# Down projection in pairs of output tiles: seven block products over ten of 22 K tiles, and the moves of the turned results issued by GpSimd

## Chip, cores and metric

The kernel runs on one core of a Trainium2 chip. The metric is the device time of one launch in microseconds; lower is better.

## What is computed

One layer of a hybrid decoder over 512 prompt tokens and 32 sample tokens (8 sequences of 4), 544 tokens in all, in fp32: attention and a recurrent branch, merged and projected, then an RMS norm and a SwiGLU block. The change is in the last product of that block and in what follows it:

```
f = rmsnorm(x, g_ffn_pre)
g_, u_ = jnp.split(f @ w_gate_up, 2, axis=-1)
x = x + rmsnorm((jax.nn.silu(g_) * u_) @ w_down, g_ffn_post)
```

Here D_MODEL is 1024 and D_FF is 2816, so that `w_down` has 22 K tiles of 128 rows (KF) and 8 output tiles of 128 columns (KD).

## The kernel before

**Products.** Activations stand transposed, features on the partitions and the 544 tokens on the columns, cut into two halves of 272 (HT). Every fp32 operand is split into a high part rounded to fp32r and the low rest; a product is three matmuls, high by high, high by low and low by high (weights first). ScalarE makes the high part with a copy (`hi`, L1501), VectorE the low part with a subtraction (`lo`, L2021).

**Gate and up stage.** It already multiplies in blocks: each of NS = 20 column pairs of gate and up takes seven products of 2x2 blocks instead of eight (`product`, L1364; `gu_period` on ScalarE L1896 and VectorE L2479; `sum_5`, `sum_76`, `sum_3` make the weight sums). The products are written on 128x272 PSUM banks, and VectorE and ScalarE add and copy between them. Its result is `hid`, 22 tiles of 128x544. In the last period VectorE also splits the first two pieces of the down weights and begins with `hid_low`, which makes the low part of a hidden tile (L2443); `hid_high` (L1876) makes the high part.

**Down stage.** Each of the eight output tiles m takes 22 K tiles x 3 matmuls x 2 halves = 132 matmuls (`down`, `down_steps`, L1428). The weights of a tile come in three pieces of 8, 8 and 6 K tiles (DOWN_K) through a ring of two slots: SyncE loads (`load_down`), ScalarE and VectorE split (`down_hi`, `down_lo`), each counted by `w_in_slot`, `hi_done`, `lo_done` and `tile_done`. Tile 0 begins before the last product of the gate and up stage, and consumes the hidden tiles as they are split. Tiles 1 to 6 are a loop over pairs. Tile 7 is written out by hand in two column parts, of 288 and 256 (LAST_CUT), so that the first part's norm, turn and store begin under the second's matmuls.

**What follows a tile.** ScalarE takes the finished tile out of PSUM in a blocked order, scaled by the norm's weight, and squares it (`y_evacuate`, L1935 to L1940). VectorE turns it in blocks of 32x32 into `yz` (`y_square`, L2527) and adds the squares. SyncE then moves the turned rows to their places in `ytok` by twelve DMAs a tile: eight for the prompt, each of 256 runs of 128 bytes, four for the samples (`move_y`, L800 and L802). Two buffers `yz` alternate, so `y_square(m)` waits until the moves of tile m-2 have landed (the semaphore starts at 16, and each tile adds 192):

```python
                if not isinstance(m, int):
                    e.wait_ge(y_moved, m * 192 - 176)
                e.transpose(yz[s][:, :], yg[s][:, :]).then_inc(y_turned, 1)
```

At the end TensorE sums the squares over the features, ScalarE takes the root, and VectorE makes the output rows, token on the partition, in two halves (L2564), after `x1_back` (the residual rows, which GpSimd reads back at L960) and after the moves of tiles 0 to 6 (`y_moved`). SyncE stores them. SyncE's queue is in order: a load of weights stands behind the moves ahead of it, and the other way round.

## Time and profile before

| | us |
|---|---|
| median of three runs | 769.75 (769.42 to 770.26) |
| the profiled execution | 768.84 |
| its span, first to last instruction | 766.70 |
| TensorE matmul busy | 757.5, 99% |
| VectorE busy | 484.2, 63% |
| ScalarE busy | 357.0, 47% |
| GpSimd busy | 70.5, 9% |
| matmuls | 5954 |
| TensorE's mean granted clock | 0.997 of 2.4 GHz |

The profile is of one execution of its own. Its times are from the span's start. PE is TensorE's matmul row, PEld its weight loads, DVE VectorE, ACT ScalarE, POOL GpSimd, SP SyncE. A matmul's row is 0.29 us long but the next one begins before it ends, so the pace is read from many in a row, not from one row's length.

### The profile page before, as it was taken

Reading aid. Unit: us, or ns where it says so; the run is one execution under the profiler, and the core shown is the slowest. Engines: PE = TensorE matmul, PEld = TensorE weight load, DVE = VectorE, ACT = ScalarE, POOL = GpSimd, SP = SyncE. Lnnn points to the kernel's source line nnn. Section 1 sums busy time; section 2 is a strip of 40 time slices with the busy share of each in tenths; the row PEclk is TensorE's granted clock in tenths of the full one; section 3 lists DMA queues with packets and bytes.
Section 4 is the critical chain, followed back from the end, with each engine's and each line's share of the span. In section 5 each row is a group of like instructions: output and inputs, shape, how many; then the busy total and the mean of one; then the engine's idle time right before and its main releaser. Section 6 shows DMA issues by size and latency. Waiting matters only on the chain.

```text
span 766.7 us, 16315 instructions
## 1 busy us (share of the span) xinstructions
PE 757.5 (99%) x5954; PEld 718.4 (94%) x5954; DVE 484.2 (63%) x760; ACT 357.0 (47%) x627; POOL 70.5 (9%) x156
## 2 busy tenths in 40 slices
PE   8999999999999999999999999999999999999996
PEld 6989899899898899987899999999999999999996
DVE  7456838647656555773569887777877786232323
ACT  7334634634634632343556555554555564223322
POOL 6602102011120110021000000000000010000000
PEclk9999999999999999999999999999999999999998
DMA  9645656445454225525460333332233134434333
GB/s 263 169 110 117 162 131 139 128 104 135 129 134 104 61 74 168 175 70 181 160 194 6 106 109 109 109 108 81 85 109 109 55 127 138 107 91 111 93 91 127
DMA packets 196979, 91.68 MB, mean 120 GB/s; under 512 B 65143, under 2 KB 190539, under 8 KB 196941
## 3 DMA queue, kind: packets, MB, share of 16 engines
q1 hardware_dynamic: 193182, 84.36, 40.3%
q0 software_dynamic: 2576, 6.45, 2.5%
q8 instruction: 24, 0.39, 0.2%
q10 hardware_dynamic: 1182, 0.35, 0.2%
q14 instruction: 15, 0.11, 0.1%
HBM read 82.37 MB, written 6.81 MB: 116 GB/s over the span
## 4 chain that ended last, share of the span: by engine, by line
PE 97%; DMA 1%; POOL 1%; DVE 0%; DVEq 0%; issue 0%; ACT 0%; POOLq 0%
PE ps L975 34%; PE ps L1364 28%; PE ps L1428 17%; PE ps L1258 6%; PE ps L1332 3%; PE ps L1181 2%; PE ps L1082 1%; PE ps L1096 1%; PE ps L1114 1%; DMA strow<-in_state_h_dram 1%; PE ps L1156 1%; PE ps L1266 1%; PE ps L1067 1%; PE ps L1127 1%; POOL prow L833 0%; PE ps L1293 0%
## 5 line engine op out<-in xcount | busy, mean ns | idle before, releaser
L2021 DVE TENSOR_TENSOR w_lo<-w_raw,w_hi 128x1024 fp32r<-128x1024 f32 (+1 forms) x65 | 77.3, 1190 | 120.5 <-ACT w_hi L1501 120.2
L1501 ACT ACTIVATE w_hi<-w_raw 128x1024 fp32r<-128x1024 f32 (+1 forms) x66 | 67.8, 1029 | 122.2 <-PE ps L1428 78.1
L975 PE MATMUL ps<-xin_hi,w_hi 128*128 128x272 f32 x544 | 117.0, 296 | 0.0
L975 PE MATMUL ps<-xin_hi,w_lo 128*128 128x272 f32 x544 | 112.5, 288 | 0.0
L975 PE MATMUL ps<-xin_lo,w_hi 128*128 128x272 f32 x544 | 112.3, 288 | 0.0
L975 PEld LDWEIGHTS ps<-xin_hi,w_hi 128*128 128x128 f32 x544 | 84.8, 188 | 8.1 <-issue 7.6
L975 PEld LDWEIGHTS ps<-xin_lo,w_hi 128*128 128x128 f32 x544 | 85.4, 188 | 0.0
L975 PEld LDWEIGHTS ps<-xin_hi,w_lo 128*128 128x128 f32 x544 | 85.0, 189 | 0.0
L1428 PE MATMUL ps<-hid_hi,w_hi 128*128 128x272 f32 (+2 forms) x352 | 75.3, 289 | 0.0
L1428 PE MATMUL ps<-hid_lo,w_hi 128*128 128x272 f32 (+2 forms) x352 | 74.9, 287 | 0.0
L1428 PE MATMUL ps<-hid_hi,w_lo 128*128 128x272 f32 (+2 forms) x352 | 74.9, 287 | 0.0
L1428 PEld LDWEIGHTS ps<-hid_lo,w_hi 128*128 128x128 f32 x352 | 56.2, 188 | 0.0
L1428 PEld LDWEIGHTS ps<-hid_hi,w_hi 128*128 128x128 f32 x352 | 55.8, 188 | 0.0
L1428 PEld LDWEIGHTS ps<-hid_hi,w_lo 128*128 128x128 f32 x352 | 55.8, 188 | 0.0
L1364 PE MATMUL ps<-xq_lo,b_hi 128*128 128x272 f32 x160 | 46.6, 292 | 0.0
L1364 PE MATMUL ps<-xq_hi,a_lo 128*128 128x272 f32 x160 | 46.4, 290 | 0.0
L1364 PE MATMUL ps<-xq_lo,a_hi 128*128 128x272 f32 x160 | 46.2, 289 | 0.0
L1364 PE MATMUL ps<-xq_hi,b_hi 128*128 128x272 f32 x160 | 46.2, 288 | 0.0
L1364 PE MATMUL ps<-xq_hi,b_lo 128*128 128x272 f32 x160 | 46.1, 288 | 0.0
L1364 PE MATMUL ps<-xq_hi,c_hi 128*128 128x272 f32 x160 | 46.1, 288 | 0.0
L1364 PE MATMUL ps<-xq_hi,a_hi 128*128 128x272 f32 x160 | 46.1, 288 | 0.0
L1364 PE MATMUL ps<-xq_hi,c_lo 128*128 128x272 f32 x160 | 45.9, 287 | 0.0
(349 smaller groups left out, 1769.0 us busy)
## 6 DMA issues: line engine op xcount, KB each, us to landing
w_raw<-in_w_in_dram SPq DMA_DIRECT2D x68, 256.0 KB, 3.2
g_raw<-in_w_gate_up_dram SPq DMA_DIRECT2D x40, 256.0 KB, 3.7
w_raw<-in_w_down_dram SPq DMA_DIRECT2D x40, 256.0 KB, 2.8
u_raw<-in_w_gate_up_dram SPq DMA_DIRECT2D x20, 256.0 KB, 3.0
e_raw<-in_w_gate_up_dram SPq DMA_DIRECT2D x20, 256.0 KB, 4.2
kc<-in_cache_k_dram SPq DMA_DIRECT2D x64, 64.0 KB
vc<-in_cache_v_dram SPq DMA_DIRECT2D x64, 64.0 KB
wo_raw<-in_w_out_dram SPq DMA_DIRECT2D x12, 256.0 KB, 4.0
```

Of the source, the lines that this page charges most:

```text
L975: mm = e.matmul(ps[:, bank + h, 0:HT], wt[:, kw, :], xt[:, kx, h * HT:h * HT + HT], start=first and wt is wh and xt is xh, stop=last and ( ...
L1067: e.matmul(ps[GR * g:GR * g + GR, S_BANK, 0:PAST], q_bd[:, b, :], kcT[:, b, :], start=b < NG, stop=b >= NG, skip_group_check=True)
L1082: mm = e.matmul(ps[:, SCORE_BANK[h], score_cols(qt)], qT[rows, qt * P:(qt + 1) * P], kT[rows, 0:(qt + 1) * P], start=True, stop=True)
L1096: mm = e.transpose(ps[:, T_BANK, c0:c0 + P], lgt[:, h, l0 + kt * P:l0 + kt * P + P], ident[:, :])
L1114: mm = e.matmul(ps[DH * h:DH * h + DH, O_BANK, kt * P:SEQ], tok[:, 1, kt, DH * h:DH * h + DH], value_cols(h, kt), start=kt == 0, stop=kt = ...
L1181: mm = e.matmul(ps[:, 2 * s + h, 0:cols.stop - cols.start], w[:, k, :], x[:, k, cols], start=first and k == 0, stop=last and k == KD - 1, ...
L1258: mm = e.matmul(ps[:, o_bank(tt) + c, :], xt[:, k, tt * P:tt * P + P], wt[:, c * NHALF:(c + 1) * NHALF], start=k == K_ORDER[0] and xt is x ...
L1332: mm = e.matmul(ps[:, 4 * m + 2 * c + h, 0:HT], wt[:, k, :], xt[:, x, k % KQ, :], start=k == 0 and wt is wh and xt is xq_hi, stop=k == KD ...
L1364: mm = e.matmul(ps[:, bank, 0:HT], wt[:, k0 + k, :], xt[:, x, k, :], start=first and k == 0 and wt is wh and xt is xq_hi, stop=last and k ...
L1428: mm = e.matmul(ps[:, D_BANK[odd] + h, 0:cols.stop - cols.start], wt[:, k, :], x, start=first and k == ks[0] and wt is wh and not lo_x, st ...
L1501: e.activation((to or w_hi[s])[:, 0:k, :], w_raw[s][:, 0:k, :], ACT.Copy).then_inc(hi_done, count)
L2021: e.tensor_tensor(wl[:, 0:k, :], w_raw[s][:, 0:k, :], wh[:, 0:k, :].bitcast(F32), ALU.subtract).then_inc(lo_done, count)
```

## The change

Tiles 1 to 6 are made in three pairs (N7). K tiles 6 to 10 (from KA) and 11 to 15 (from KB), five each (SK), two output tiles and two column halves make blocks of 2x2, which take seven products instead of eight. Four sums of hidden blocks (`hs`) are made once, in and after the last period of the gate and up stage; four sums of weight blocks (`op_sums`) are made for each pair on VectorE, in place in the raw buffers. The other 12 K tiles stay plain and are added into the same banks, in four pieces of three K tiles for each output tile. A pair has 15 operands (OPS7): seven of five K tiles, eight of three, all split into one ring of three slots (`op_hi`, `op_lo`), whose slot j % 3 may be written when operand j-3 has been used. The raw plain pieces have two buffers. ScalarE copies four partial results out of PSUM (`snap`), VectorE adds five times (`c_11`, `c_21_part`, `c_12`, `c_22_21`), and the tile is taken from `c_pair` in SBUF (`y_pair`) instead of from PSUM. The loops over pairs are unrolled.

SyncE keeps the weight loads: four of five K tiles (320 KB) and eight of three (192 KB) a pair, in place of six pieces in two DMAs each. The `move_y` DMAs go to GpSimd's queue. The reads of x1 rows, which GpSimd issued in a row after the gate and up stage, now stand among the moves and wait for late operands of the third pair. `y_moved` no longer starts at 16, and `y_square(m)` waits for the moves of tiles 0 to m-1. Tiles 0 and 7 keep their matmuls; tile 7's pieces come under new counts (C_LAST).

```diff
+SK, KA, KB = 5, 6, 11
+PLAIN_K, PK = (0, 3, 16, 19), 3
+N7 = (KD - 2) // 2
+OPS7 = 15
+(OP_A11, OP_A12, OP_A22, OP_P1, OP_S2, OP_S3, OP_S1, OP_S4, OP_P2) = (0, 1, 2, 3, 7, 8, 9, 10, 11)
+C_LAST = C_DOWN + 3
+HS_0, OP_0, SUM_0, C_0 = 4, KD, 3 * NS, NS
...
+            def load_op(n, op, buf, k0, m):
+                e.dma_start(buf[:, :, :], wd[:, k0:k0 + SK, m * P:m * P + P]).then_inc(raw_in[op], 16)
+            def load_plain(n, i):
+                r = 8 * n + i
+                k0, m = PLAIN_K[i % 4], 2 * n + 1 + i // 4
+                e.dma_start(raw_p[r % 2][:, :, :], wd[:, k0:k0 + PK, m * P:m * P + P]).then_inc(raw_p_in[r % 2], 16)
+            e.wait_ge(lo_done, C_DOWN + 4)
+            load_op(0, "11", raw_11, KA, 1)
+            e.wait_ge(q2_done, NS)
+            load_plain(0, 0)
+            e.wait_ge(lo_done, C_DOWN + 5)
+            load_op(0, "12", raw_12, KB, 1)
+            load_op(0, "22", raw_22, KB, 2)
+            e.wait_ge(tile_done, C_DOWN + 5)
+            load_op(0, "21", raw_21, KA, 2)
+            load_plain(0, 1)
+            for n in range(N7):
+                o = OPS7 * n
+                for i in (2, 3, 4, 5):
+                    e.wait_ge(op_l, OP_0 + o + OP_P1 + i - 1)
+                    load_plain(n, i)
+                if n + 1 < N7:
+                    e.wait_ge(op_sum, SUM_0 + 4 * n + 4)
+                    e.wait_ge(op_l, OP_0 + o + OP_S2 + 1)
+                    load_op(n + 1, "11", raw_11, KA, 2 * n + 3)
+                    e.wait_ge(op_l, OP_0 + o + OP_S3 + 1)
+                    load_op(n + 1, "21", raw_21, KA, 2 * n + 4)
+                    e.wait_ge(op_l, OP_0 + o + OP_S1 + 1)
+                    load_op(n + 1, "22", raw_22, KB, 2 * n + 4)
+                    e.wait_ge(op_l, OP_0 + o + OP_S4 + 1)
+                    load_op(n + 1, "12", raw_12, KB, 2 * n + 3)
+                else:
+                    e.wait_ge(op_sum, SUM_0 + 4 * N7)
+                    e.wait_ge(op_l, OP_0 + o + OP_S4 + 1)
+                    for c in range(2):
+                        k0 = sum(DOWN_K[:c])
+                        load(C_LAST + c, (1 + c) % 2, wd[:, k0:k0 + DOWN_K[c], (KD - 1) * P:KD * P], DOWN_K[c])
+                for i in (6, 7):
+                    e.wait_ge(op_l, OP_0 + o + OP_P2 + i - 5)
+                    load_plain(n, i)
+                if n + 1 < N7:
+                    for i in (0, 1):
+                        e.wait_ge(op_l, OP_0 + o + OP_P2 + i + 3)
+                        load_plain(n + 1, i)
+            load(C_LAST + 2, 1, wd[:, KF - DOWN_K[2]:KF, (KD - 1) * P:KD * P], DOWN_K[2])
...
+            for m in range(KD - 3):
+                for part in range(3):
+                    move_y(m, m % 2, part)
+            e.wait_ge(op_used, OP_0 + OPS7 * (N7 - 1) + OP_S1 + 1)
+            for tt in (1, 2, 3):
                 e.dma_start(x1tok[:, tt, :], token_rows(x1_dram, tt)).then_inc(x1_back, 16)
+            for part in range(3):
+                move_y(KD - 3, 1, part)
+            e.wait_ge(op_used, OP_0 + OPS7 * N7 - 1)
+            e.dma_start(x1tok[:, 0, :], token_rows(x1_dram, 0)).then_inc(x1_back, 16)
             e.dma_start(x1tok[0:TS, TT, :], x1_dram[SEQ:T, :]).then_inc(x1_back, 16)
+            for part in range(3):
+                move_y(KD - 2, 0, part)
...
+            def block_product(n, j, bank, x, first, last):
+                e.wait_ge(op_l, OP_0 + OPS7 * n + j + 1)
+                wh, wl = op_hi[j % 3], op_lo[j % 3]
+                for k, (xh, xl) in enumerate(x):
+                    for wt, xt in ((wh, xh), (wh, xl), (wl, xh)):
+                        mm = e.matmul(ps[:, bank, 0:HT], wt[:, k, :], xt, start=first and k == 0 and wt is wh and xt is xh,
+                                      stop=last and k == SK - 1 and wt is wl, skip_group_check=True)
+                mm.then_inc(op_used, 1)
+            def plain_rest(n, j0, banks, firsts, lasts):
+                for i, k0 in enumerate(PLAIN_K):
+                    j = j0 + i
+                    e.wait_ge(op_l, OP_0 + OPS7 * n + j + 1)
+                    wh, wl = op_hi[j % 3], op_lo[j % 3]
+                    for k in range(PK):
+                        for wt, lo_x in ((wh, False), (wh, True), (wl, False)):
...
+                    mm.then_inc(op_used, 1)
...
+            for n in range(N7):
+                if n > 0:
+                    e.wait_ge(c_snap, C_0 + 4 * n)
+                block_product(n, OP_A11, U_BANK, hid_block(KA, 0), True, True)
+                if n > 0:
+                    e.wait_ge(c_done, C_0 + 5 * n - 4)
+                block_product(n, OP_A12, C11_BANK, hid_block(KB, 0), True, False)
+                if n > 0:
+                    e.wait_ge(c_done, C_0 + 5 * n)
+                e.wait_ge(hs_l, HS_0 + 1)
+                block_product(n, OP_A22, C21_BANK, sum_block(3), True, False)
+                if n > 0:
+                    e.wait_ge(c_done, C_0 + 5 * n - 2)
+                plain_rest(n, OP_P1, (C11_BANK, C12_BANK), (False, True), (True, False))
+                e.wait_ge(hs_l, HS_0 + 2)
+                e.wait_ge(c_snap, C_0 + 4 * n + 1)
+                block_product(n, OP_S2, U_BANK, sum_block(1), False, True)
+                e.wait_ge(hs_l, HS_0 + 3)
+                block_product(n, OP_S3, C22_BANK, sum_block(2), True, True)
+                e.wait_ge(hs_l, HS_0 + 4)
+                e.wait_ge(c_snap, C_0 + 4 * n + 2)
+                block_product(n, OP_S1, U_BANK, sum_block(0), False, True)
+                block_product(n, OP_S4, C12_BANK, hid_block(KB, 1), False, True)
+                e.wait_ge(c_snap, C_0 + 4 * n + 3)
+                plain_rest(n, OP_P2, (C21_BANK, C22_BANK), (False, False), (True, True))
...
-            e.wait_ge(y_free, KD)
+            e.wait_ge(c_done, C_0 + 5 * N7 - 2)
...
+            def op_high(n, j):
+                o = OPS7 * n + j
+                if o < 2:
+                    e.wait_ge(tile_done, C_DOWN + 4)
+                elif o == 2:
+                    e.wait_ge(tile_done, C_DOWN + 5)
+                else:
+                    e.wait_ge(op_used, OP_0 + o - 2)
+                if OP_P1 <= j < OP_S2 or j >= OP_P2:
+                    r = 8 * n + (j - OP_P1 if j < OP_S2 else j - OP_P2 + 4)
+                    e.wait_ge(raw_p_in[r % 2], raw_p_0[r % 2] + 16 * (r // 2 + 1))
+                    e.activation(op_hi[j % 3][:, 0:PK, :], raw_p[r % 2][:, :, :], ACT.Copy).then_inc(op_h, 1)
+                else:
+                    if j in (OP_A11, OP_A12, OP_A22):
+                        op = {OP_A11: "11", OP_A12: "12", OP_A22: "22"}[j]
+                        e.wait_ge(raw_in[op], raw_0[op] + 16 * n + 16)
+                    else:
+                        e.wait_ge(op_sum, SUM_0 + 4 * n + {OP_S1: 1, OP_S3: 2, OP_S2: 3, OP_S4: 4}[j])
+                    e.activation(op_hi[j % 3][:, :, :], raw_of(j)[:, :, :], ACT.Copy).then_inc(op_h, 1)
+            def snap(n, use, j, dst, bank):
+                e.wait_ge(op_used, OP_0 + OPS7 * n + j + 1)
+                if n > 0:
+                    e.wait_ge(c_done, C_0 + 5 * n)
+                e.activation(dst, ps[:, bank, 0:HT], ACT.Copy).then_inc(c_snap, 1)
...
+            hs_high(3, 4)
+            op_high(0, 0); op_high(0, 1)
+            hs_high(1, 4)
+            op_high(0, 2); op_high(0, 3)
+            hs_high(2, 4)
+            op_high(0, 4)
+            hs_high(0, 4)
+            for n in range(N7):
+                if n > 0:
+                    op_high(n, 2); op_high(n, 3)
+                snap(n, 1, OP_A11, c_pair[0][:, 0:HT], 2)
+                if n == 0:
+                    op_high(n, 5)
+                    y_evacuate(0, 0)
+                else:
+                    y_pair(2 * n, 0, c_pair[1], 5 * n)
+                    op_high(n, 4); op_high(n, 5)
+                for j in range(6, 10):
+                    op_high(n, j)
+                snap(n, 2, OP_S2, c_pair[1][:, 0:HT], 2)
+                op_high(n, 10)
+                snap(n, 3, OP_S3, p7_snap[:, :], 5)
+                op_high(n, 11)
+                snap(n, 4, OP_S1, c_pair[1][:, HT:T], 2)
+                op_high(n, 12); op_high(n, 13)
+                y_pair(2 * n + 1, 1, c_pair[0], 5 * n + 3)
+                op_high(n, 14)
+                if n + 1 < N7:
+                    for j in range(2):
+                        op_high(n + 1, j)
+            e.wait_ge(op_used, OP_0 + OPS7 * N7 - 1)
+            hi(C_LAST, C_LAST // 2, 1, DOWN_K[0])
+            e.wait_ge(op_used, OP_0 + OPS7 * N7)
+            hi(C_LAST + 1, (C_LAST + 1) // 2, 0, DOWN_K[1])
+            y_pair(KD - 2, 0, c_pair[1], 5 * N7)
+            hi(C_LAST + 2, (C_LAST + 2) // 2, 1, DOWN_K[2])
...
+            b11, b12 = (hid[:, KA:KA + SK, h * HT:h * HT + HT] for h in range(2))
+            b21, b22 = (hid[:, KB:KB + SK, h * HT:h * HT + HT] for h in range(2))
             q = NS - 1
+            e.wait_ge(hid_done, KB + SK)
+            e.wait_ge(a_l, NS)
+            e.tensor_tensor(hs[0][:, :, :], b12, b11, ALU.subtract).then_inc(hs_done, 1)
             up_2(q - 1, 0)
+            e.wait_ge(hs_done, HS_0 + 1)
+            e.tensor_tensor(hs[1][:, :, :], b22, hs[0][:, :, :], ALU.subtract).then_inc(hs_done, 1)
             low_b(q)
             low_c(q, 1)
             gate_1(q, 1)
-            for c in range(2):
-                lo(C_DOWN + c, c)
+            e.wait_ge(c_l, NS)
+            e.tensor_tensor(hs[2][:, :, :], b22, b12, ALU.subtract).then_inc(hs_done, 1)
             up_1(q - 1, 0)
+            lo(C_DOWN, 0)
             low_d(q, 1)
             hid_product(q - 1, hid[:, KF - 2, :])
             for k in range(2):
                 hid_low(k)
+            lo(C_DOWN + 1, 1)
             up_2(q, 1)
-            for k in range(2, EARLY):
+            for k in range(2, 4):
                 hid_low(k)
             up_1(q, 1)
+            e.wait_ge(hs_done, HS_0 + 2)
+            e.wait_ge(d_l, NS)
+            e.tensor_tensor(hs[3][:, :, :], b21, hs[1][:, :, :], ALU.subtract).then_inc(hs_done, 1)
+            for k in range(4, EARLY):
+                hid_low(k)
+            e.wait_ge(hs_done, HS_0 + 4)
+            hid_low(EARLY)
             hid_product(q, hid[:, KF - 1, :])
...
...
+            def op_sums(n):
+                e.wait_ge(raw_in["21"], raw_0["21"] + 16 * n + 16)
+                e.wait_ge(op_l, OP_0 + OPS7 * n + OP_A22 + 1)
+                e.tensor_tensor(raw_22[:, :, :], raw_21[:, :, :], raw_22[:, :, :], ALU.add).then_inc(op_sum, 1)
+                e.wait_ge(op_sum, SUM_0 + 4 * n + 1)
+                e.tensor_tensor(raw_21[:, :, :], raw_11[:, :, :], raw_21[:, :, :], ALU.subtract).then_inc(op_sum, 1)
+                e.wait_ge(op_sum, SUM_0 + 4 * n + 2)
+                e.tensor_tensor(raw_11[:, :, :], raw_22[:, :, :], raw_11[:, :, :], ALU.subtract).then_inc(op_sum, 1)
+                e.wait_ge(op_sum, SUM_0 + 4 * n + 3)
+                e.tensor_tensor(raw_12[:, :, :], raw_12[:, :, :], raw_11[:, :, :], ALU.subtract).then_inc(op_sum, 1)
...
             def y_square(m, s):
                 e.wait_ge(y_free, m + 3)
-                if not isinstance(m, int):
-                    e.wait_ge(y_moved, m * 192 - 176)
+                if m > 1:
+                    e.wait_ge(y_moved, m * 192)
                 e.transpose(yz[s][:, :], yg[s][:, :]).then_inc(y_turned, 1)
...
+            op_low(0, 0)
+            op_low(0, 1)
+            hs_low(3, 1)
+            op_low(0, 2)
+            op_low(0, 3)
+            hs_low(1, 2)
+            op_low(0, 4)
+            op_sums(0)
+            op_low(0, 5)
+            e.memset(yacc[:, :], 0.0).then_inc(consts_v, 1)
+            e.wait_ge(consts_v, 7)
             y_square(0, 0)
-            with e.Fori(0, (KD - 2) // 2) as n:
-                y_tile(n, 1)
-                y_tile(n + 1, 0)
-            lo(C_DOWN + 3 * KD - 1, (C_DOWN + 3 * KD - 1) % 2, DOWN_K[2])
+            op_low(0, 6)
+            hs_low(2, 3)
+            op_low(0, 7)
+            hs_low(0, 4)
+            for n in range(N7):
+                if n > 0:
+                    c_22_21(n - 1)
+                    op_low(n, 2); op_low(n, 3)
+                    op_sums(n)
+                    op_low(n, 4); op_low(n, 5)
+                    y_square(2 * n, 0)
+                    op_low(n, 6); op_low(n, 7)
+                c_11(n)
+                op_low(n, 8); op_low(n, 9); op_low(n, 10)
+                c_21_part(n)
+                op_low(n, 11); op_low(n, 12); op_low(n, 13)
+                c_12(n)
+                op_low(n, 14)
+                y_square(2 * n + 1, 1)
+                if n + 1 < N7:
+                    op_low(n + 1, 0); op_low(n + 1, 1)
+            lo(C_LAST, 1, DOWN_K[0])
+            c_22_21(N7 - 1)
+            lo(C_LAST + 1, 0, DOWN_K[1])
+            y_square(KD - 2, 0)
+            lo(C_LAST + 2, 1, DOWN_K[2])
```

## Rows read from the trace of the kernel before

**Rows 1.** The page's table of busy time, whole span.

```profile
PE 757.5 (99%) x5954; PEld 718.4 (94%) x5954; DVE 484.2 (63%) x760; ACT 357.0 (47%) x627; POOL 70.5 (9%) x156
```

**Rows 2.** The chain that ended last, in order of time: start, length, what.

```profile
413.57 208.33 PE ps L1364 x1656
...
623.42 3.00 PE ps L1364 x24
626.42 127.52 PE ps L1428 x1014
```

**Rows 3.** Waits, 620 to 766: total, times, longest.

```profile
ACT w_hi L1501 <- PE ps L1428: 78.1, 21, 5.2
...
DVE yz L2527 <- DMA ytok<-yz: 2.8, 4, 0.7
```

**Rows 4.** Timeline of VectorE, 596 to 642.

```profile
601.16 1.22 DVE L2400 TENSOR_TENSOR b_lo<-s_raw,b_hi 128x1024 fp32r<-128x1024 f32 x1
602.30 1.22 DVE L2400 TENSOR_TENSOR c_lo<-e_raw,c_hi 128x1024 fp32r<-128x1024 f32 x1
...
608.74 0.72 DVE L2436 TENSOR_TENSOR hid<-sl,ub 128x544 f32 x1
611.37 0.44 DVE L2422 SCALAR_TENSOR_TENSOR ub<-ub,ps 128x272 f32<-128x272 f32 x1 [1.91 <-PE ps L1364]
...
628.28 6.44 DVE L2443 TENSOR_TENSOR hid_lo<-hid,hid_hi 128x544 fp32r<-128x544 f32 x10
...
635.51 3.90 DVE L2443 TENSOR_TENSOR hid_lo<-hid,hid_hi 128x544 fp32r<-128x544 f32 x6
```

**Rows 5.** Timeline, TensorE and ScalarE: start, length, instruction, idle before.

```profile
559.72 0.29 PE L1364 MATMUL ps<-xq_hi,a_lo 128*128 128x272 f32 x1
...
560.05 0.40 ACT L1855 ACTIVATE gh<-ps 128x272 f32<-128x272 f32 x1 [0.40 <-PE ps L1364]
...
626.75 5.57 ACT L1876 ACTIVATE hid_hi<-hid 128x544 fp32r<-128x544 f32 x10
...
637.06 1.06 ACT L1501 ACTIVATE w_hi<-w_raw 128x1024 fp32r<-128x1024 f32 x1 [0.72 <-PE ps L1428]
```

**Rows 6.** DMA issues: count, size of one, median from issue to landing.

```profile
w_raw<-in_w_down_dram SPq DMA_DIRECT2D x40, 256.0 KB, 2.8
...
ytok<-yz SPq DMA_DIRECT2D x56, 32.0 KB, 2.1
...
bias_rev<-dist_shift POOLq DMA_DIRECT2D x4, 130.0 KB, 3.3
...
dist_shift<-drow POOLq DMA_DIRECT2D x4, 8.1 KB, 4.3
```

**Rows 7.** Instructions of DMA issues, SyncE's with ns min/median/max, GpSimd's with mean ns.

```profile
L800 SPq DMA_DIRECT2D ytok<-yz x56: 631/638/1180, 645.4 to 749.9; - x56
L802 SPq DMA_DIRECT2D ytok<-yz x28: 529/579/648, 657.2 to 752.5; - x28
...
L816 SPq DMA_DIRECT2D out_dram<-ytok x4: 341/364/376, 757.5 to 763.5; - x4
...
L856 POOL DMA_DIRECT2D bias_rev<-dist_shift x4 | 2.1, 554 | 4.0 <-DMA dist_bias<-drow 4.0
L960 POOL DMA_DIRECT2D x1tok<-x_dram x4 | 2.1, 528 | 252.2 <-PE ps L1364 252.2
...
L852 POOL DMA_DIRECT2D dist_shift<-drow x4 | 2.0, 509 | 1.3 <-ACT drow L1545 1.3
```

**Rows 8.** Timeline of ScalarE and VectorE at the end.

```profile
741.93 0.74 ACT L1935 ACTIVATE yg<-ps,prm 128x256 f32<-128x256 f32 x1
...
743.21 0.64 ACT L1940 ACTIVATE ysq<-ps 128x544 f32<-128x544 f32 x1
...
756.21 3.67 DVE L2564 SCALAR_TENSOR_TENSOR ytok<-ytok,ycol,x1tok 128x1024 f32<-128x1024 f32 x3 [0.47 <-DVE ycol L2557]
...
761.01 2.48 DVE L2564 SCALAR_TENSOR_TENSOR ytok<-ytok,ycol,x1tok 128x1024 f32<-128x1024 f32 x2 [0.34 <-ACT ytok L1968]
```

More of the change, by code:

```diff
@@ new lines, in _, with hs_low @@
+            e.wait_ge(d_l, NS)
[4 more added lines that the diff above has]
+            hid_low(EARLY)
+            hid_product(q, hid[:, KF - 1, :])
+            def hs_low(i, count):
+                e.wait_ge(hs_h, HS_0 + count)
+                e.tensor_tensor(hs_lo[i][:, :, :], hs[i][:, :, :], hs_hi[i][:, :, :].bitcast(F32), ALU.subtract).then_inc(hs_l, 1)
```

184 lines of the change are left out of this document (117 added, 67 removed).

## The prediction

> **What bounds the kernel now.** I read the page's table of busy time first: TensorE's matmul row is busy 99% of the span [rows 1], at full clock throughout. Then the chain that ended last, in order of time: from 413.57 it is matmuls only, one block of 1656 and, in the down stage, one of 1014 without a break in 127.52 us [rows 2]. That is 125.8 ns a matmul in both (208.33 / 1656 and 127.52 / 1014), whether neighbours change the PSUM bank or stay on it. The waits of the down stage say who waits for whom: ScalarE waits for TensorE, VectorE for ScalarE, and in tile after tile VectorE's 32x32 turn waited for the moves of the turned rows, 2.8 us in four times, which cost nothing because TensorE had work [rows 3]. So a matmul less is 125.8 ns less, as long as its operand is split in time; and a move of turned rows costs nothing only as long as nobody on the path waits for it.
>
> **Matmuls.** Tiles 1 to 6 take 2 x 22 x 6 = 264 matmuls a pair. Now a pair takes 7 x 5 x 3 = 105 in block products and 8 x 3 x 3 x 2 = 144 plain ones, 249. Three pairs: 45 fewer, 45 x 0.1258 = 5.66 us. Tiles 0 and 7 keep theirs.
>
> **The other engines' prices.** VectorE: 1024 columns 1.22 us, 544 columns 0.72, 272 columns 0.44 [rows 4], so 1.04 ns a column and 0.15 to begin; two independent ones follow each other 0.08 under that. A block operand (640 columns) is 0.82, a plain one (384) 0.55, a sum of hidden blocks (1360) 1.57. ScalarE: 1024 columns 1.06, and ten of 544 in 5.57 [rows 5]: 0.73, 0.51 and 1.35 for the same three. From the last matmul of a product to ScalarE's start I take 0.2 us from the product's last issue slot: matmul at 559.72 for 0.29, ScalarE at 560.05 [rows 5]. Per pair VectorE has 15 operands (9.1), four weight sums (each waits for the last, 4 x 0.86), five adds from the products (1.8), two turns and adds (2.8): 17 of 31.3 us. ScalarE has some 13. Neither is the bound by its sum; only order can hurt.
>
> **Front of the stage.** VectorE gets four sums of 1.57. The first fits between 609.46 and 611.37, where it was idle [rows 4]; the others push what follows. Worked forward: the second ends at 613.3, two operands and an add later the third at 617.5; an add, a piece, an operand, a product, two low parts, a piece, an add and two low parts bring VectorE to 624.3; the next add waits for its matmuls until 625.1, the fourth sum ends at 627.0, three low parts at 628.9. So the last hidden product starts 2 us later than before, at 628.9, and the low part of hidden tile 7 lands at 630.3, where TensorE wants it at 626.42 + 5 x 0.755 = 630.2 [rows 2, 4]: a stall of 0.1. After that VectorE makes a tile each 0.64 and TensorE eats one each 0.755, so the lateness isn't repeated. Bounds: 0 (the sums fall in idle time) and 0.9 (one more wait of VectorE there). I take 0.1.
>
> **Inside a pair.** Split operands go round three slots: ScalarE may make operand j when product j-3 has ended, and TensorE then has two products to do, 3.8 to 4.5 us, against 0.73 + 0.82 + 0.3 of latency. About 2 us are left for what stands before it in the two in-order queues. The tightest place is the ninth operand (index 8): VectorE first adds C11, which needs the end of product 6; 0.2 + 0.36 + 0.82 + 0.04 = 1.4 after it, inside product 7's 1.89: 0.5 to spare. The four weight sums (3.45) sit before operand 4, with 0.9 to spare. Raw weights: a plain piece is 192 KB, the nearest load row is 256 KB in 2.8 us [rows 6]; I take 2.6, and 3.2 for 320 KB; the plain pieces would have to land 1.6 later than that before TensorE waited. So 0 here; bounds 0 and 2.5 (each pair waits once for 0.8).
>
> **The step to the last tile.** ScalarE's first piece of tile 7 waits until the last but one product has been used, then 1.06 + 1.22 and latencies of 0.27 = 2.55 against that last product's 2.26: 0.3 stall. TensorE's sum: -5.66 + 0.1 + 0.3 = -5.3.
>
> **The moves.** Twelve DMAs a tile leave SP's queue (there 0.638 and 0.579 us of issue each, 2.1 to landing) and go to GpSimd's, in a fixed order with the x1 reads. SP had room, so nothing on the path gains by that; SP now carries 15 loads a pair and none of its waits is late in the schedule above. The trace has no such move from GpSimd. Nearest rows: 8 rows a DMA 0.509, 128 rows 0.528 to 0.554 [rows 7]. The prompt moves have 256 runs of 128 bytes; by those rows they are 0.58, the four sample moves 0.51. Upper bound: SP takes 0.364 for 128 long rows and 0.638 for such a move [rows 7]; the same factor 1.75 on 0.528 gives 0.92 (and 0.8 for the small ones). Lower: 0.53. Landing: 3.3 for 130 KB into SBUF, 4.3 for small ones into HBM [rows 6]; lower 2.9 (3.3 less the 0.3 or 0.4 by which SP's moves beat its 256 and 128 KB loads). I take 3.3. GpSimd's x1 issues at 626.7, beside VectorE's busiest stretch, took the same 0.53 [rows 7], so I charge nothing for VectorE beside them.
> Q, from a turn to the last of its moves landed, is then 8 x 0.58 + 3 x 0.51 + 3.3 = 9.5 us.
>
> The change also makes each turn wait until all moves of the tile right before have landed (before, those of the tile before that one: the count went from m*192 - 176 with 16 given in advance to m*192 with none). Odd to even tile is the short way: in the schedule tile 1's turn ends at 669.5 and tile 2's is due at 680.3, 10.8 for Q = 9.5. It holds, barely. If it fails, the operand queued behind the turn (index 6, a plain one) is late only after 3.2 more, since VectorE idles 1.6 there and TensorE wants it 1.6 later still.
>
> **The end** is where it doesn't hold. Tile 5's turn ends at 732.9: its plain operand 13 waits for a piece issued behind four loads of tile 7, then add, ScalarE's copies of 1.28 + 0.64 [rows 8], one operand, turn. Moves landed 742.4; only then tile 6's turn, 743.1 (its data are ready at 738.6); moves landed 743.1 + 9.5 = 752.6. The last piece of tile 7 is split by VectorE behind that turn, done 744.6, wanted 745.1: no stall. The final adds of the first half stood at 756.21 and would stand at 750.9 with TensorE's 5.3; they wait for the moves instead, until 752.65. They take 3.67, so the second half starts at 756.35, where it stood at 761.01 and TensorE would have let it start at 755.7 [rows 8]. 1.1 us of the moves' 1.7 are hidden by the slack between 756.21 + 3.67 and 761.01. End: -4.65.
>
> The Trainium skill, DMA: Bandwidth & Descriptors, section Issuing engines are not separate DMA queues, says that issuing from several engines saves only sequencer time, since all share the DMA engines; the rows agree in that SP's time wasn't on the path, and the sum has no gain for it.
> The same page, Anatomy of one DMA, puts a GpSimd DMA at 2.0 us plus bytes / 436e3, an estimate of 2.1 for 32 KB; with the 0.58 of issue that would make the landing 2.7, Q 8.9, and the whole -5.3.
>
> **Sum.** The profiled execution took 768.84 us (span 766.70); the median of the three timed runs is 769.75, 0.9 more. 769.75 - 4.65 = 765.1 us.
>
> **Rivals.**
> A. TensorE alone sets the end: the moves land in time (Q up to 9.1). For it: GpSimd's 0.53 and SP's short landing; against: landings of 3.3 and 4.3 [rows 6]. -5.3, 764.4 (764.2 to 765). Chance 0.22.
> B, mine: Q between 9.1 and 10.9 and the moves eat part of the gain: -5.2 to -1.8, 764.6 to 768. Chance 0.48.
> C. Waits inside the pairs: landing of raw pieces later by 1.6 or more, or an order that costs one wait of 0.8 or so a pair, 2.5 in all on top of B: -2.1, 767.6 (766 to 769). Against: schedule slack of 0.5 to 2.8 at every operand. Chance 0.12.
> D, other side: GpSimd's issue is as much dearer as SP's was, 0.92 and 0.8. Q = 7.4 + 2.4 + 3.3 = 13.1. The even tiles' turns wait 2.3 us, inside their 3.2; at the end the two Qs stand one behind the other: 732.9 + 13.1 + 0.8 + 13.1 + 3.7 = 763.6 for the second half against 761.0: +2.6, 772.3 (with landings of 4.3, 2 more: 774.3). It decides from Q = 11.8 on, where 732.9 + 2Q + 0.8 + 3.7 reaches 761.0. For it: no row has 256 runs from GpSimd. Against: from 8 to 128 rows the price rose by 4 to 9%. Chance 0.14.
> E. The gain isn't there (matmuls slow down by new operands or the longer code without a loop): long unlooped stretches ran at the same pace earlier, 0 to +1. Chance 0.04.
>
> **Numbers.** A difference under 0.2% (1.5 us) can hardly be told from none. Faster by more than that (under 768.2): A, nearly all of B and two thirds of C, 0.76. Same (to 771.3): a little of B, the rest of C, E and the mildest D, 0.10. Slower 0.14. The range 763.9 to 770.0 holds A, B, C and part of E; B's own is 764.6 to 768. The lower end is the bound with no stall at all (-5.66, 764.1) less the runs' scatter; above 770.0 stand D and a bit of E, 0.16.
>
> **What would show it.** Right: 5909 matmuls, 45 fewer, the chain still TensorE's up to some 753; GpSimd busy with 84 moves of 0.5 to 0.6 us; VectorE's turn of tile 6 waiting 4 us for a DMA; the first final add waiting for a DMA (about 1.7 us) and starting near 752.6; tile 7's first matmul after a gap of 0.3. Wrong: moves of 0.8 us or more from GpSimd, with waits of TensorE after each even tile's turn (C and D differ by who is waited for: a load's or a move's DMA), or a matmul pitch over 126 ns.

## The result, and the profile after

The changed kernel takes 772.16 us (median, 770.59 to 773.85) against 769.31 (768.92 to 773.07) of the kernel before on the same chips: ratio 1.0034, 95% interval 1.0028 to 1.0041. It is slower by 2.85 us; 765.1 was predicted, with a range up to 770.0. The profiled execution of the changed kernel took 772.7 us (span 770.9), 0.5 over its median. The one of before lay 0.5 under the median of its 22 runs, so the two traces stand 3.9 apart (4.2 in span) and not 2.85.

The page's table of busy time of the changed kernel, which answers to [rows 1]: 45 matmuls fewer, as counted, and TensorE busy for 2.3 us less, where 5.66 were expected.

```profile
PE 755.2 (98%) x5909; PEld 715.4 (93%) x5909; DVE 519.2 (67%) x822; ACT 376.1 (49%) x670; POOL 125.1 (16%) x240
```

The chain that ended last, in order of time (start, length, what), which answers to [rows 2]. L1531 are the products of tiles 0 and 7, L1569 the block products, L1584 the plain ones.

```profile
622.36 1.51 PE ps L1531 x12
623.87 3.00 PE ps L1467 x24
626.87 15.27 PE ps L1531 x120
642.14 5.63 PE ps L1569 x45
...
673.38 5.63 PE ps L1569 x45
...
704.62 5.63 PE ps L1569 x45
710.25 9.06 PE ps L1584 x72
719.31 1.90 PE ps L1569 x15
...
725.24 9.98 DMA raw_p<-in_w_down_dram
735.30 0.53 ACT op_hi L2105
735.86 0.57 DVE op_lo L2769
736.47 7.47 PE ps L1584 x36
743.95 13.00 PE ps L1531 x102
```

The first and the second pair take 31.24 us each (642.14, 673.38, 704.62), which is 249 matmuls at 125.5 ns, without a stall. The third takes 39.33 (704.62 to 743.95): 8.1 us are lost in it. The chain names the place: one plain weight piece, issued at 725.24, is under way for 9.98 us, and behind it stand its two splits and then TensorE.

The waits from 620 to 770 (total, times, longest), which answer to [rows 3]. ScalarE waited for that one load, VectorE for ScalarE, TensorE for VectorE:

```profile
DVE op_lo L2769 <- ACT op_hi L2105: 30.9, 14, 9.5
ACT op_hi L2105 <- DMA raw_p<-in_w_down_dram: 21.7, 7, 9.5
...
PE ps L1584 <- DVE op_lo L2769: 5.1, 1, 5.1
```

The timeline of TensorE around the stall (one row is two matmuls), and the windows of 5 us beside it (after the length: busy time of TensorE, of its weight loads, of VectorE, ScalarE and GpSimd, then the granted clock as a share of 2.4 GHz, the busy share of the DMA engines, and GB/s):

```profile
730.68 0.41 PE L1584 MATMUL ps<-hid_lo,op_hi 128*128 128x272 f32 x2
730.93 0.41 PE L1584 MATMUL ps<-hid_hi,op_lo 128*128 128x272 f32 x2
736.47 0.82 PE L1584 MATMUL ps<-hid_hi,op_hi 128*128 128x272 f32 x2 [5.13 <-DVE op_lo L2769]
737.09 0.66 PE L1584 MATMUL ps<-hid_lo,op_hi 128*128 128x272 f32 x2
737.55 0.66 PE L1584 MATMUL ps<-hid_hi,op_lo 128*128 128x272 f32 x2
...
742.53 0.42 PE L1584 MATMUL ps<-hid_lo,op_hi 128*128 128x272 f32 x2
742.78 0.41 PE L1584 MATMUL ps<-hid_hi,op_lo 128*128 128x272 f32 x2
```

```profile
725.00:730.00 5.00, 5.00 (x42) 5.00 (x41) 0.56 (x1) 0.81 (x2) 1.61 (x3) 1.00 0.88 242
730.00:735.00 5.00, 1.35 (x11) 1.12 (x9) 0.00 (x0) 0.00 (x0) 0.00 (x0) 1.00 0.83 313
735.00:740.00 5.00, 3.53 (x15) 3.53 (x16) 1.60 (x4) 3.00 (x7) 0.00 (x0) 0.57 0.03 9
740.00:745.00 5.00, 5.00 (x33) 5.00 (x32) 3.14 (x5) 2.07 (x3) 3.88 (x6) 0.75 0.19 44
```

The 8.1 us are two things. TensorE stands for 5.3 us (from 731.18, when the two matmuls of 730.93 have left their slots, to 736.47). Then a pair of matmuls takes 0.45 us instead of 0.25 until 742.5, while the granted clock is at the lower level (1.2 GHz; 0.50 in each window of 1 us from 736 to 742); the 26 matmuls from 736.47 to 742.53 take 6.1 us instead of 3.3, which is the other 2.8. The DMA columns say what went on meanwhile: the engines were busy at 0.88 and 0.83 of their share, where the 5 us ahead of these show 0.16.

Who filled them stands in the timeline of the two issuing queues:

```profile
723.18 2.02 SPq L650 DMA_DIRECT2D w_raw<-in_w_down_dram  x4
725.24 1.56 SPq L849 DMA_DIRECT2D raw_p<-in_w_down_dram  x2
```

```profile
725.26 1.61 POOL L1057 DMA_DIRECT2D x1tok<-x_dram  x3 [4.46 <-PE ps L1569]
```

SyncE issued four loads of tile 7 (256 KB each) and, 0.02 us ahead of GpSimd, the first of two plain pieces; GpSimd issued three reads of x1 (512 KB each), which the kernel before had issued at 626.72, ahead of all of this. Nine transfers, 2.9 MB, were issued from 723.18 to 726.9. Both plain pieces took 10.0 and 10.1 us, where the median of the 24 is 2.6.

The moves, as instructions (ns min/median/max) and as transfers (count, size, median to landing), which answer to [rows 7] and [rows 6]:

```profile
L1048 POOL DMA_DIRECT2D ytok<-yz x56: 702/707/743, 652.9 to 757.5; - x56
L1050 POOL DMA_DIRECT2D ytok<-yz x28: 496/512/533, 658.5 to 759.7; - x28
```

```profile
raw_p<-in_w_down_dram SPq DMA_DIRECT2D x24, 192.0 KB, 2.6
raw<-in_w_down_dram SPq DMA_DIRECT2D x12, 320.0 KB, 3.2
...
ytok<-yz POOLq DMA_DIRECT2D x56, 32.0 KB, 2.0
ytok<-yz POOLq DMA_DIRECT2D x28, 4.0 KB, 1.6
```

And the end, from the timeline of VectorE, which answers to [rows 8]:

```profile
749.88 0.74 DVE L2808 STREAM_TRANSPOSE yz<-yg 128x544 f32<-128x544 f32 x1 [3.58 <-DMA ytok<-yz]
...
761.41 3.66 DVE L2869 SCALAR_TENSOR_TENSOR ytok<-ytok,ycol,x1tok 128x1024 f32<-128x1024 f32 x3 [2.67 <-DMA ytok<-yz]
...
765.19 2.48 DVE L2869 SCALAR_TENSOR_TENSOR ytok<-ytok,ycol,x1tok 128x1024 f32<-128x1024 f32 x2
```

The sum over the two traces: the last square sums of TensorE begin at 762.56, where they stood at 759.55: 3.0 later, which is -5.66 for the matmuls, +0.2 for the front (15.27 for 120 matmuls), +8.1 for the third pair and +0.5 because the down stage began later (622.36 for 621.90), in all 3.1. The last adds stand at 765.19 against 761.01: 1.2 more than TensorE's 3.0, because the first adds had waited for the moves.

### The profile page after: what moved, and what is told of

Read it like the earlier page. It is cut to its first block, busy times and chain, and to the rows that moved or that the text cites. A ratio compares the mean times of both kernels' runs of the same rounds, so it can differ in the third digit from the quotient of the medians.

```text
span 770.9 us, 16112 instructions
## 1 busy us (share of the span) xinstructions
PE 755.2 (98%) x5909; PEld 715.4 (93%) x5909; DVE 519.2 (67%) x822; ACT 376.1 (49%) x670; POOL 125.1 (16%) x240
## 4 chain that ended last, share of the span: by engine, by line
PE 95%; DMA 2%; POOL 1%; DVE 1%; ACT 0%; SPq 0%; issue 0%; DVEq 0%; POOLq 0%; ACTq 0%
PE ps L1078 33%; PE ps L1467 27%; PE ps L1584 7%; PE ps L1361 6%; PE ps L1569 4%; PE ps L1531 4%; PE ps L1435 3%; PE ps L1284 1%; PE ps L1185 1%; PE ps L1199 1%; DMA raw_p<-in_w_down_dram 1%; PE ps L1217 1%; DMA strow<-in_state_h_dram 1%; PE ps L1259 1%; PE ps L1369 1%; PE ps L1170 1%
## 5 line engine op out<-in xcount | busy, mean ns | idle before, releaser
L1048 POOL DMA_DIRECT2D ytok<-yz x56 | 39.4, 710 | 324.4 <-DVE yz L2808 321.6
L2247 DVE TENSOR_TENSOR w_lo<-w_raw,w_hi 128x1024 fp32r<-128x1024 f32 (+1 forms) x47 | 56.9, 1211 | 51.4 <-ACT w_hi L1664 51.1
L1664 ACT ACTIVATE w_hi<-w_raw 128x1024 fp32r<-128x1024 f32 (+1 forms) x48 | 50.1, 1045 | 51.4 <-PE ps L1078 39.5
L1467 PE MATMUL ps<-xq_lo,c_hi 128*128 128x272 f32 x160 | 45.9, 287 | 0.0
L1584 PE MATMUL ps<-hid_hi,op_hi 128*128 128x272 f32 x144 | 31.1, 299 | 5.1 <-DVE op_lo L2769 5.1
L2769 DVE TENSOR_TENSOR op_lo<-raw_p,op_hi 128x384 fp32r<-128x384 f32 x24 | 13.2, 556 | 30.9 <-ACT op_hi L2105 30.9
L1986 ACT ACTIVATE a_hi<-g_raw 128x1024 fp32r<-128x1024 f32 x20 | 21.2, 1062 | 21.1 <-PE ps L1467 17.5
L1584 PE MATMUL ps<-hid_lo,op_hi 128*128 128x272 f32 x144 | 30.8, 296 | 0.0
```

What stands on the lines that cost most here:

```text
L1048: e.dma_start(prompt[:, 2 * part:2 * part + 2, d, :], yz[s][rows, c0:c0 + 2 * P]).then_inc(y_moved, 16)
L1467: mm = e.matmul(ps[:, bank, 0:HT], wt[:, k0 + k, :], xt[:, x, k, :], start=first and k == 0 and wt is wh and xt is xq_hi, stop=last and k ...
L1584: mm = e.matmul(ps[:, banks[h], 0:HT], wt[:, k, :], x, start=firsts[h] and i == 0 and k == 0 and wt is wh and not lo_x, stop=lasts[h] and ...
L1664: e.activation((to or w_hi[s])[:, 0:k, :], w_raw[s][:, 0:k, :], ACT.Copy).then_inc(hi_done, count)
L1986: e.activation(a_hi[:, :, :], g_raw[s][:, :, :], ACT.Copy).then_inc(a_h, 1)
L2247: e.tensor_tensor(wl[:, 0:k, :], w_raw[s][:, 0:k, :], wh[:, 0:k, :].bitcast(F32), ALU.subtract).then_inc(lo_done, count)
```

## The experiments

Each is compared with the kernel before, run on the same chip. Theory T: the plain piece is late because the three reads of x1 that the change puts within the third pair (the early reads, below) and tile 7's loads are in the DMA engines with it. Rivals: SyncE's order alone (R1), the moves on GpSimd (R2). The first four kernels:

**e1_order.** The last two plain pieces are issued ahead of tile 7's loads.

```
-                else:
+                for i in (6, 7):
+                    e.wait_ge(op_l, OP_0 + o + OP_P2 + i - 5)
+                    load_plain(n, i)
+                if n + 1 == N7:
                     e.wait_ge(op_sum, SUM_0 + 4 * N7)
-                    e.wait_ge(op_l, OP_0 + o + OP_S4 + 1)
                     for c in range(2):
                         ...
-                for i in (6, 7):
-                    e.wait_ge(op_l, OP_0 + o + OP_P2 + i - 5)
-                    load_plain(n, i)
```

> The changed kernel, with SyncE issuing plain pieces 6 and 7 of the third pair ahead of the first four loads of tile 7. Nothing else. Theory T (the 1.5 MB of x1 reads that GpSimd issues at 725.3 and the 1 MB of tile 7 together fill the DMA engines, and whatever weight load is behind them is late): piece 6, issued before the reads, lands in 3 us, piece 7 in 5 to 7, and now tile 7's first piece is late: TensorE stalls 1 to 3 us at the step to tile 7 or at the last operand; 766 to 768.5 us. Rival R1 (only the order in SyncE's queue matters, the x1 reads do no harm): no stall over 0.5, about 764.5. Rival R2 (moves on GpSimd are what costs): little changes, 771 to 772.

768.51 us (768.02 to 769.17), ratio 0.9987 (0.9978 to 0.9996). The stall of 5.3 is gone. Three remain: 0.47 early in the pair (at 716.4), 1.85 because the second of the two pieces still took 7.6 us beside the reads, and 0.64 at the step to tile 7. The clock kept its level. The first final adds waited 3.4 us for the moves. TensorE's stalls are T's; the time is at the upper end of what T had said.

**e2_reads.** The three early reads of x1 go behind the moves of tile 5, with the fourth.

```
-            e.wait_ge(op_used, OP_0 + OPS7 * (N7 - 1) + OP_S1 + 1)
-            for tt in (1, 2, 3):
-                e.dma_start(x1tok[:, tt, :], ...)
...
-            e.dma_start(x1tok[:, 0, :], ...)
+            for tt in (0, 1, 2, 3):
+                e.dma_start(x1tok[:, tt, :], ...)
```

> The changed kernel, with GpSimd's x1 reads of rows 1, 2 and 3 issued after the moves of tile 5, beside the read of rows 0, so that none is in flight beside the third pair's pieces. Nothing else. T: the 1 MB of tile 7 alone ahead of piece 6; it lands in 3.5 to 4.5 us instead of 10, TensorE stalls less than 0.7 us before operand 13, and the clock stays at 2.4 GHz: about 8 us off the changed kernel, 764 to 765.5. R1: piece 6 still lands after 7 us or more, a stall of 3 or more, 767 to 770. R2: 771 to 772.

772.70 us (771.3 to 773.33), ratio 1.0039 (1.0026 to 1.0053). The two pieces landed in 4.1 and 4.8 us, TensorE lost 0.7 there and 0.5 within tile 7, and yet the time didn't fall: the first final adds now waited 6.3 us for the moves of tile 6. The landing and the stall are T's; the time isn't, and lies even above R2's.

**e3_both.** Both edits.

> Both edits together. T and R1: no stall in the third pair, its 249 matmuls in 31.3 us as in the others; the end limited by the moves of tiles 5 and 6; 764 to 765.5, at most 0.7 better than with the reads moved alone under T. R2: 771 to 772.

768.67 us (768.13 to 769.25), ratio 0.9989 (0.9980 to 0.9998). TensorE is as predicted: the only gap left is 0.3 at the step to tile 7, and its last square sums begin at 754.43, 5.1 before the 759.55 of the kernel before. But the time is lower by 0.6 only, where 764 to 765.5 had been expected. GpSimd's timeline shows where the gain went:

```profile
739.98 2.14 POOL L1058 DMA_DIRECT2D x1tok<-x_dram  x4
742.10 0.50 POOL L1059 DMA_DIRECT2D x1tok<-x_dram  x1
742.91 3.53 POOL L1047 DMA_DIRECT2D ytok<-yz  x5 [0.30 <-issue]
751.75 2.10 POOL L1047 DMA_DIRECT2D ytok<-yz  x3 [5.32 <-issue]
753.85 2.02 POOL L1049 DMA_DIRECT2D ytok<-yz  x4
```

After the fifth move of tile 6, GpSimd issues nothing for 5.32 us, and the profile names no semaphore ("issue"). The adds waited 6.3 us for the moves.

**e4_before_pool.** The kernel before, with its 84 moves on GpSimd behind the reads of x1, and each turn waiting for all tiles ahead of it: R2 alone.

> The kernel before (no block products, loops and ring as they were), with its 84 moves issued by GpSimd behind the x1 reads, and the turn of tile m waiting for the moves of all tiles before it, as in the change. T: moves of 0.71 and 0.51 us, landed 8.8 us after the turn, 11 us or more before the next turn: no wait on the path, the first final add within 0.5 us of where it was, 769 to 770. R2: the time is 1 us or more above before (770.5 to 772).

769.31 us (768.82 to 772.46), ratio 1.0004 (0.9994 to 1.0013). The moves cost the same 0.709 and 0.514 us there, and no turn waits for them. A stop of 2.5 us within tile 6's moves shows here too, and the first final adds waited 1.4 us for the moves, which the end hid. (The profiled execution took 772.46, the longest of the eleven: its gate and up stage had begun 3.8 us later, at 417.39 for 413.57.)

So T holds, with both of its parts, for the third pair, and R2 is out for it. The order matters, and alone gives back 3.6 us (ratio 0.9987 for 1.0034), but R1 said more, that the reads do no harm, and a piece that took 7.6 us ahead of tile 7's loads speaks against it. For the end R2 isn't out: once TensorE is early, its gain is lost in waits for moves that GpSimd issues. What stays open is the stop of GpSimd. The next four kernels are about it and about the size of T:

**f1_last_sp.** e3, and tile 6's moves are issued by SyncE, on a semaphore of their own.

```
-            for part in range(3):          (GpSimd)
-                move_y(KD - 2, 0, part)
+            for part in range(3):          (SyncE, behind tile 7's last load)
+                move_y(KD - 2, 0, part)    (increments y_moved6)
```

> Both edits of e3 (the last plain pieces issued ahead of tile 7's loads, the four large reads of x1 behind the moves of tile 5), and tile 6's twelve moves are issued by SyncE instead of GpSimd, on a semaphore of their own. In e3 TensorE ended 5.1 us earlier than in the kernel before, but GpSimd stopped for 5.3 us within tile 6's moves, and the final add waited 6.3 us for them. Theory H (GpSimd's issue stands still at one place of its own sequence of DMAs until its own transfers in flight have landed, and that alone eats the gain of e3): SyncE has no such stop, tile 6's moves are through some 8 us after its turn (eight at 0.64 and four at 0.58 by SyncE's rows of before), ahead of TensorE's end, so the final add waits for TensorE alone; 769.3 - 5.1 + 0.1 = 764.3 us, ratio 0.9935. Rival G (the moves are slow because 2 MB of reads are in the DMA engines ahead of them, whoever issues): the moves land as late as in e3, about 756.9, and the time stays at 768.7, ratio 0.999.

764.84 us (764.52 to 765.79), ratio 0.9942 (0.9928 to 0.9955). SyncE issued the twelve moves from 741.84 to 751.98, without a stop but with single issues of up to 1.5 us, so that they took 10.1 us and not the 8 that had been expected, and the adds still waited 2.4 us.

**f2_reads_sp.** e1, and all reads of x1 are issued by SyncE behind tile 7's last load.

> The order edit of e1, and all five reads of x1 issued by SyncE behind tile 7's last load; GpSimd issues only the 84 moves. Theory H: the stop of GpSimd's issue within tile 6's moves waits for GpSimd's own transfers, and the reads are no longer among them, so that it is 2.5 us or less (as in e4, where GpSimd had its reads long before); the second half of tile 6's moves starts about 749 and lands by 754; total 764.5 to 766 us, ratio 0.994 to 0.996. Rival G (transfers of anyone in the DMA engines hold it): the stop stays at 5 us or more beside the 2 MB of reads, and the time is again about 768.7.

770.22 us (769.26 to 771.32), ratio 1.0004 (0.9993 to 1.0014): neither theory's number. The stop did shrink to 2.5 us, as H had said, but the reads now began while tile 5's moves were still on their way. The last of these, issued by 741.01, had landed only at 747.2. VectorE's turn of tile 6 waited for it, and the last split of tile 7 stood behind that turn in VectorE's order. The timelines of VectorE and of TensorE, then TensorE's windows:

```profile
747.25 0.74 DVE L2807 STREAM_TRANSPOSE yz<-yg 128x544 f32<-128x544 f32 x1 [8.39 <-DMA ytok<-yz]
747.91 0.68 DVE L2809 TENSOR_TENSOR yacc<-yacc,ysq 128x544 f32<-128x544 f32 x1
748.52 0.95 DVE L2246 TENSOR_TENSOR w_lo<-w_raw,w_hi 128x768 fp32r<-128x768 f32 x1
```

```profile
745.82 0.29 PE L1530 MATMUL ps<-hid_hi,w_lo 128*128 128x288 f32 x1
749.52 0.61 PE L1530 MATMUL ps<-hid_hi,w_hi 128*128 128x288 f32 x1 [3.41 <-DVE w_lo L2246]
```

```profile
750.00:755.00 5.00, 5.00 (x23) 5.00 (x23) 0.00 (x0) 0.75 (x2) 3.54 (x6) 0.50 0.22 43
```

**f3_reads_sp_relax.** f2, with two semaphores for the moves, so that the turn of tile m waits for tile m-2 alone.

```
-                    e.wait_ge(y_moved, m * 192)
+                    e.wait_ge(y_moved[m % 2], m // 2 * 192)
```

> As the run with all reads on SyncE, and with two semaphores for the moves, by the parity of the tile, so that the turn of tile m waits for the moves of tile m-2 alone and not for all before it. In e3 the turn of tile 6 waited for tile 5's moves to about 742; without that wait it would come at about 738, and tile 6's moves as GpSimd comes to them, right behind tile 5's. Theory H: 764.3 us if the stop is 2.5 us or less, since the moves are then 2 us further ahead of TensorE's end; with a stop of 5 us (rival G) still about 767.

763.90 us (763.54 to 765.36), ratio 0.9931 (0.9915 to 0.9946), the best of all: 5.6 us under the kernel before. The turn of tile 6 came at 738.93, TensorE has no gap but the 0.3, the stop lasted 1.8 us, and the final adds waited for moves no more.

**f4_one_read.** The changed kernel with one early read of x1 instead of three.

> The changed kernel with its own order on SyncE, and with one large read of x1 (512 KB) at the early place instead of three; the other three go with the fourth behind tile 5's moves. With none early (e2) the sixth plain piece of the third pair landed in 4.1 us, with three in 10.1 us. Theory T (the piece lands behind all bytes that are in the engines, so its landing grows with them in proportion): about 6.1 us, TensorE stands about 2.6 us or less at that place and the granted clock keeps its level or falls only briefly. Rival R1 (it is SyncE's order alone, and e2's gain was the missing GpSimd issue): 4.1 us, no longer than with none. Time about 771 to 772 by the stop of GpSimd, not used.

774.37 us in that one execution. The two pieces landed in 6.5 and 6.7 us (4.1 and 4.8 with no early read, 10.0 and 10.1 with three): near T's 6.1, not R1's 4.1. TensorE stood 1.8 and 1.1 us in the pair and 0.6 within tile 7, at the full clock. The time is that of a single execution and isn't used.

The last four kernels ask what is left beyond f1, and what the stop is bound to:

**g1_best.** f1, and f3's two semaphores (tile 6's moves on SyncE count on a third, `raw_in["11"]`).

> The run with tile 6's moves on SyncE (764.84), and the two semaphores by parity, so that the turn of tile 6 no longer waits 3.3 us for tile 5's moves. SyncE's twelve moves then start about 2 us earlier and are landed by some 751, so that the first three adds of the end start with their sums (750.8 in the run with the reads on SyncE) and not 2.4 us after; what ends last is then TensorE's last square sums and the second pair of adds. Theory: 763.9 us less at most 0.5, ratio about 0.992. Rival: the 2 MB of reads and the moves of tiles 5 and 6 now meet in the DMA engines, the moves of tile 6 land as late as before, and the time stays at 764.8.

764.66 us (764.46 to 765.52), ratio 0.9943 (0.9929 to 0.9956): no better than f1, as the rival said. SyncE's moves began 1.8 us earlier, but one of the small ones took 1.88 us of issue, and the adds still waited 1.3.

**g2_again.** e3, and GpSimd issues tile 0's twelve moves twice.

```
+                if m == 0:
+                    e.wait_ge(y_moved, 192)
+                    for part in range(3):
+                        move_y(0, 0, part, y_again)
```

The turns from tile 2 on wait for `y_again` too.

> e3, and GpSimd issues the twelve moves of tile 0 twice (the second time the same bytes to the same place, where GpSimd is idle), so that its sequence of DMAs is twelve longer ahead of tile 5. Hypothesis H1 (the stop sits at one place of GpSimd's own sequence): with no reads before it, it came after the seventh move of tile 6 (79 moves), so it now comes after the seventh move of tile 5, where only small moves are in flight and it lasts 2.5 us or less; tile 6's moves go without a stop, and the time is 764.5 to 766 us. H2 (the stop comes from the traffic of that moment): it stays at tile 6's moves and lasts 5 us, 768.7 us.

765.18 us (764.66 to 765.77), ratio 0.9945 (0.9931 to 0.9958). Twelve DMAs more, and 3.5 us less than e3. But the stop isn't after the seventh move of tile 5, where H1 had put it; it is nowhere to be seen.

**h1_four.** The same with the four small moves only.

> e3, and GpSimd issues only the four small moves of tile 0 (4 KB each) a second time, instead of all twelve. If the stop of GpSimd's issue sits at a count of its DMAs, it comes four moves earlier than in e3, after the first move of tile 6 instead of the fifth, and still waits for the reads just issued: 5 us or more, 768.7 us or a little more. If it sits at an amount of rows moved (four small moves have 128 rows of 128 bytes, half of one large move's 256), it comes at most one move earlier, 768.7 us. If it comes from neither, twelve moves more having only shifted it out by chance of timing, it stays after the fifth.

764.56 us (763.93 to 771.17, the last a single one of ten; the next is 765.87), ratio 0.9948 (0.9928 to 0.9967). None of the three ways that had been expected: the stop is gone, though only four DMAs were added. The same place in GpSimd's timeline, with eight moves in a row where e3 had five and a stop:

```profile
740.65 2.16 POOL L1062 DMA_DIRECT2D x1tok<-x_dram  x4
742.77 0.53 POOL L1063 DMA_DIRECT2D x1tok<-x_dram  x1
743.27 5.63 POOL L1048 DMA_DIRECT2D ytok<-yz  x8
748.89 2.02 POOL L1050 DMA_DIRECT2D ytok<-yz  x4
```

**h2_pad.** e3, and 96 satisfied waits in GpSimd's program instead of DMAs (48 instructions more were executed).

> e3 with 96 waits that are already satisfied added in GpSimd's program behind the moves of tile 0, and no DMA more. If the stop sits at a place of GpSimd's code, it leaves the fifth move of tile 6: earlier, where the reads are not in flight, and the time falls to 764.5 to 766 us as in the run with twelve moves more. If it sits in the sequence of DMAs alone, it stays after the fifth move, 5.3 us, and the time stays at 768.7 us.

768.43 us (767.88 to 769.89), ratio 0.9991 (0.9981 to 1.0001): the stop stays after the fifth move, 4.98 us long.

```profile
743.40 3.53 POOL L1047 DMA_DIRECT2D ytok<-yz  x5 [0.28 <-issue]
751.92 2.10 POOL L1047 DMA_DIRECT2D ytok<-yz  x3 [4.98 <-issue]
```

Whether the stop comes thus depends on the DMAs that GpSimd has issued before it, and neither on the length of its program nor on the reads in flight, which GpSimd issues right ahead of tile 6's moves in e3, h1 and g2 alike. It isn't a fixed number of DMAs, though. Counted from tile 0's first move, or from the reads where these come earlier, the stop stands behind 82 DMAs where GpSimd has reads among the moves (the changed kernel, e1, e2, e3, f4, h2), behind 79 where it has none (f2, f3), and behind 84 in e4. What it waits for is less sure. It lasted 5.7, 5.3 and 5.0 us with four of GpSimd's own large reads just issued (e2, e3, h2), 4.6 with three (f4), 0.9 with one (the changed kernel, e1), and 1.8 to 2.5 with none (f3; f2, e4), each in one profiled execution. So many reads ahead of it make it long, but are not its cause. Nor does it end as soon as they have landed: in e3 it lasts from 746.44 to 751.75, and the share of busy DMA engines in windows of 2 us is 0.85 from 747, 0.10 from 749 and 0.00 from 751. Why four small DMAs remove it and don't just shift it stays open.

## Why the prediction was wrong

**Matmuls: right.** 5909, and 125.5 ns each in the pairs. The whole sum of TensorE, -5.3, came true as -5.1 in e3.

**Front of the stage, and the step to tile 7: right.** 0.2 for 0.1; and in e3, where nothing hides the step, 0.3 for 0.3.

**Inside a pair: the step that failed.** "I take 2.6 [...] the plain pieces would have to land 1.6 later than that before TensorE waited. So 0 here; bounds 0 and 2.5." In the third pair the piece that TensorE stood for landed 7.4 later than 2.6. By the prediction's own slack that is 5.8 of stall, and 5.3 was measured; the clock, which the prediction had in no term, added 2.8. So this term was 8.1 where 0 had been taken and 2.5 was the bound. The median of the 24 pieces was right (2.6) and was taken for each of them, without asking what else is in the DMA engines at that one. The reads of x1, which the change moves from the front of the stage into the third pair, were named only for their place in GpSimd's order, and tile 7's loads only for theirs ahead of the piece on SyncE's; their 2.5 MB were in no sum. Rival C had the right kind of wait but priced it as one of 0.8 in every pair, 2.5 in all: it missed by a factor of three because it was one large wait in one pair, and it had no clock in it. A step that is moved takes its bytes along: at 626.72 the reads had met no tight load, at 725.26 they met the tightest. The price by bytes can be read off the runs: 4.8 us without an early read, 6.7 with one, 10.1 with three, about 1.8 us for 512 KB, which fits the 242 and 313 GB/s of the windows.

The Trainium skill, DMA: Bandwidth & Descriptors, section Issuing engines are not separate DMA queues, says that the DMAs of all issuing engines interleave on the same 16 engines. The prediction took from it only that there is no gain in a second queue; the other half, that GpSimd's reads stand in the way of SyncE's piece, is what these landings show (10.1 us against 4.8).

**The moves: the parts off, the sum right by luck.** Issue 0.707 and 0.51 for 0.58 and 0.51, landing 2.0 and 1.6 for 3.3. The lower bound of 2.9 for the landing was misread too: SyncE's moves beat its 256 KB loads by 0.7 [rows 6], not by 0.3 or 0.4. Tile 5's moves began at 741.12 and the turn that waited for them at 749.88, 8.8 from the first issue. But the turn before had ended at 740.52, and the 0.6 from there to the first issue is in no term of the prediction, which counts Q from the turn's end. So Q was 9.4 for 9.5: dearer issue (+1.0), the short landing (-1.7) and the missing 0.6 cancel. Rival D (0.92 and 0.8) is out; its 772.3 for the 772.16 measured is a coincidence, for its prices didn't come, and the stall of TensorE that did isn't in it.

**The end: two things unforeseen.** The turn of tile 6 did wait for the moves (3.6 us, 4 had been said), and the first final adds did too. But beside large reads a move lands later than its median (6.6 us in f2, counted from the start of its issue at 740.52), and GpSimd's own stop, which no step had, stands within tile 6's moves: 0.88 us in the changed kernel, 5.3 once the reads come right ahead of it. That is why taking the stall away (e2, e3) gave nothing or little, and why f1, h1 and g2, which keep that stop off tile 6's moves, come to 764.6 to 765.2, with waits of the first final adds of 2.1 to 2.4 us where 1.7 had been predicted. The predicted 765.1 is thus the time that the change comes to without the collision and without the stop. It is not what this kernel does.

## What to carry to other kernels

A landing time taken from a median holds only where the DMA engines are as free as they were for the median: for each load with little slack, add up the bytes that any engine issues in the few us around it, at 1.8 us for 512 KB here, and give tight small loads their place ahead of bulk ones. Where an in-order engine waits for a transfer, look at what is queued behind the wait (the turn of tile 6 held tile 7's split, and that TensorE); a semaphore that waits for no more than needed went with 6.3 us from f2 to f3. When a stall that was removed leaves the time as it was, look at the last waits again before the theory is given up.
